# Sums of squares with tokens on partitions, a modulation in fewer operations, and a reordered end, in a two-layer decoder step

## What is computed

```python
def rmsnorm(x, g):
    xf = x.astype(jnp.float32)
    y = xf * lax.rsqrt(jnp.mean(xf * xf, axis=-1, keepdims=True) + EPS)
    return (y * g.astype(jnp.float32)).astype(x.dtype)

def modulate(h, shift, scale):
    return h * (1 + scale) + shift
```

## Time and profile before

| | us |
|---|---|
| runs | 1842.51, 1846.34, 1846.58 |
| median | 1846.34 |
| the profiled execution | 1857.14 |
| its span, first to last instruction | 1855.3 |
| TensorE busy | 1632.1 (88%) |
| VectorE busy | 802.2 (43%) |
| ScalarE busy | 675.4 (36%) |
| GpSimd busy | 141.8 (8%) |

### The profile page before, as it was taken

One profiled execution on the slowest core, in us unless ns is written; L12 is line 12 of the kernel. 1 busy time (PEld: TensorE's weight loads), 2 busy tenths in 40 slices (PEclk: granted clock), 3 DMA queues, 4 the chain that ended last, 5 costly groups with the idle time before them and its releaser, 6 DMA issues.

```text
span 1855.3 us, 31054 instructions
## 1 busy us (share of the span) xinstructions
PE 1632.1 (88%) x12244; PEld 1448.3 (78%) x12244; DVE 802.2 (43%) x1731; ACT 675.4 (36%) x1211; POOL 141.8 (8%) x273
## 2 busy tenths in 40 slices
PE   4698968889888999999999758999888999998996
PEld 3484457777477999998899637778577999998995
DVE  0234967677335333333353413443335333334433
ACT  2423223345214433334333323445314333334334
POOL 0311010111101000000000301111101000000000
PEclk9798569789798999999999878889888999999998
DMA  6514840002442544554131103002441222222211
GB/s 183 179 34 140 266 165 24 23 0 114 182 137 69 164 160 137 173 181 147 51 126 48 33 27 114 23 0 114 182 141 64 92 90 90 90 79 73 82 44 46
DMA packets 154361, 189.53 MB, mean 102 GB/s; under 512 B 6789, under 2 KB 148269, under 8 KB 149974
## 3 DMA queue, kind: packets, MB, share of 16 engines
q1 hardware_dynamic: 143906, 144.65, 24.5%
q0 software_dynamic: 5600, 36.24, 5.2%
q10 hardware_dynamic: 4768, 7.42, 1.2%
HBM read 183.65 MB, written 4.83 MB: 102 GB/s over the span
## 4 chain that ended last, share of the span: by engine, by line
PE 71%; DVE 12%; issue 8%; ACT 5%; DMA 2%; another core or an unknown queue 1%; ACTq 0%; DVEq 0%; POOL 0%; SPq 0%; POOLq 0%
PE ps L515 50%; PE ps L1033 3%; PE ps L1102 2%; DVE arena L949 2%; PE ps L1084 2%; DVE small L948 1%; PE ps L539 1%; PE ps L1052 1%; PE ps L598 1%; DVE arena L1263 1%; PE ps L1372 1%; PE ps L1318 1%; PE ps L1093 1%; DMA const<-in_const 1%
## 5 line engine op out<-in xcount | busy, mean ns | idle before, releaser
L515 PE MATMUL ps<-hH,wH 128*128 128x260 f32 x2592 | 535.9, 288 | 59.1 <-DVE hL L666 38.6
L515 PE MATMUL ps<-hL,wH 128*128 128x260 f32 x2592 | 529.6, 286 | 0.0
L515 PE MATMUL ps<-hH,wL 128*128 128x260 f32 x2592 | 529.6, 286 | 0.0
L515 PEld LDWEIGHTS ps<-hH,wH 128*128 128x128 f32 x2592 | 408.6, 193 | 67.1 <-issue 64.8
L499 DVE TENSOR_TENSOR wL<-ring,wH 128x1024 fp32r<-128x1024 f32 (+1 forms) x172 | 203.6, 1188 | 565.3 <-ACT wH L493 565.2
L515 PEld LDWEIGHTS ps<-hL,wH 128*128 128x128 f32 x2592 | 407.9, 192 | 0.0
L515 PEld LDWEIGHTS ps<-hH,wL 128*128 128x128 f32 x2592 | 407.5, 192 | 0.0
L493 ACT ACTIVATE wH<-ring 128x1024 fp32r<-128x1024 f32 (+1 forms) x184 | 188.8, 1029 | 584.5 <-PE ps L515 577.1
L1168 ACT ACTIVATE arena<-arena 128x128 f32<-128x128 f32 (+3 forms) x128 | 72.2, 564 | 190.2 <-DVE arena L1249 104.1
L1084 PE MATMUL ps<-arena 68*128 (+4 forms) x256 | 101.7, 488 | 8.1 <-DVE arena L1149 2.6
L1102 PE MATMUL ps<-arena 128*128 (+1 forms) x640 | 92.5, 279 | 14.9 <-ACT arena L1176 14.5
(11 more groups left out here) (258 smaller groups left out, 1804.3 us busy)
## 6 DMA issues: line engine op xcount, KB each, us to landing
ring<-in_w_ada SPq DMA_DIRECT2D x48, 1024.0 KB, 7.8
ring<-in_w_up SPq DMA_DIRECT2D x44, 1024.0 KB, 5.1
ring<-in_w_down SPq DMA_DIRECT2D x16, 1024.0 KB, 5.2
ring<-in_w_in_a SPq DMA_DIRECT2D x8, 1024.0 KB, 6.8
ring<-in_w_down SPq DMA_DIRECT2D x8, 768.0 KB, 4.6
ring<-in_w_in_b SPq DMA_DIRECT2D x6, 1024.0 KB, 5.3
ring<-in_w_o_a SPq DMA_DIRECT2D x4, 1024.0 KB, 7.8
ring<-in_w_o_b SPq DMA_DIRECT2D x4, 1024.0 KB, 10.2
```

Of the source, the lines that this page charges most:

```text
L515: ins = pe.matmul(ps[:, 2 * p + half, 0:HT], w[:, h, kc, t * P:t * P + P], mov[:, k0 + kc, half * HT:half * HT + HT], start=(first and kc ...
```

## The change

The sum of squares is turned round: a chunk's squares of 128 tokens are now the weights, and one column of ones moves, so the sums of 128 tokens land in one PSUM column, a token on each partition. 520 tokens take five such matmuls a chunk (`LANES`; the last lane overlaps). Root and reciprocal are of 128 x 5. `pe_spread` brings the reciprocals back to all partitions by multiplying with the identity. The modulation of the prompt tokens is one DVE operation with gain and reciprocal, then `hH` with the shift added on ScalarE, and `hL` in one DVE operation; the sample tokens of all chunks go together. The first panel goes chunk by chunk over both tiles. GpSimd's memsets and load are moved (`pool_fixed`): for n = 0 into the prologue, for n = 2 behind `pool_mod`. The split of the half of the second panel is issued inside the modulation (`ahead`). The residual of chunk 6 no longer waits for the last tile (`mid`). At the end GpSimd applies the gain to `xT` directly, TensorE transposes all of one half and then all of the other into seven banks, ScalarE and VectorE copy a half each with the reciprocal as scale, and SyncE stores from five buffers.

```diff
 def mm_half(pe, h, pairs, k0, nk, first, last, wait=None, mid=None):
+    if wait is None:
+        for t, p in enumerate(pairs):
+            ins = mm_tile(pe, h, t, p, k0, nk, first, last)
+            if t == 0 and mid is not None:
+                ins.then_inc(S(mid), 1)
+    else:
+        for kc in range(nk):
             wait(k0 + kc)
+            for t, p in enumerate(pairs):
+                ins = mm_chunk(pe, h, t, p, k0, kc, first and kc == 0, last and kc == nk - 1)
     ins.then_inc(S("w_used"), 1)
+LANES = (0, P, 2 * P, 3 * P, TOK - P)
 def pe_rms(pe, n, tiles=range(KC)):
     x_done(pe, n, 4)
     for kc in tiles:
+        if kc == 0:
+            pe.matmul(ps[:, 0, 0:5], zeros, ones[:, 0:5], start=True, stop=False)
         pe.wait_ge(S("rms_sq"), n * KC + kc + 1)
-        for half in range(2):
-            ins = pe.matmul(ps[:, half, 0:HT], ones[:, :], sq[:, kc % 2, half * HT:half * HT + HT],
-                            start=(kc == 0), stop=(kc == KC - 1))
+        for g, t0 in enumerate(LANES):
+            ins = pe.matmul(ps[:, 0, g:g + 1], sq[:, kc % 2, t0:t0 + P], ones[:, 0:1], start=False, stop=False)
+        if kc == KC - 1:
+            ins = pe.matmul(ps[:, 0, 0:5], zeros, ones[:, 0:5], start=False, stop=True)
         ins.then_inc(S("rms_sum"), 1)
+def pe_spread(pe, n):
+    pe.wait_ge(S("rms_ri"), n + 1)
+    for g in range(QT):
+        pe.matmul(ps[:, 6, g * P:g * P + P], rs[:, g:g + 1].to_broadcast([P, P]), ident, start=True, stop=True)
+    pe.matmul(ps[:, 7, 0:NS], rs[:, QT:QT + 1].to_broadcast([P, P]), ident[:, P - NS:P], start=True, stop=True).then_inc(S("rms_row"), 1)
 # act_rms, dve_rms
-    act.activation(v520(rt[:, :]), pair(0), ACT.Sqrt, bias=epsc[:, 0:1], scale=1.0 / D).then_inc(S("rms_rt"), 1)
-    dve.reciprocal(rt[:, :], rt[:, :]).then_inc(S("rms_ri"), 1)
+    act.activation(rs[:, 0:5], ps[:, 0, 0:5], ACT.Sqrt, bias=epsc[:, 0:1], scale=1.0 / D).then_inc(S("rms_rt"), 1)
+    dve.reciprocal(rs[:, 0:5], rs[:, 0:5]).then_inc(S("rms_ri"), 1)
+def act_mod(act, n, shift, ahead):
+    for kc in range(KC):
+        act.wait_ge(S("rms_t"), n * KC + kc + 1)
+        act.activation(hH[:, kc, 0:SEQ], hT[:, kc, 0:SEQ], ACT.Identity, bias=shift[:, kc, 0:1]).then_inc(S("rms_hi"), 1)
+        if kc == 0:
+            act.wait_ge(S("rms_s"), n + 1)
+            act.activation(hH[:, :, SEQ:TOK], hT[:, :, SEQ:TOK], ACT.Copy).then_inc(S("rms_his"), 1)
+        if kc == 6:
+            split_high(act, *ahead, 0)
+def dve_mod(dve, n, shift, ahead):
+    dve.wait_ge(S("rms_row"), n + 1)
+    dve.wait_ge(S("rms_mod"), n + 1)
+    dve.tensor_tensor(hT[:, :, SEQ:TOK], xT[:, :, SEQ:TOK], ps[:, 7, 0:NS].unsqueeze(1).to_broadcast([P, KC, NS]), ALU.mult)\
+        .then_inc(S("rms_ts"), 1)
+    for kc in range(KC + 2):
+        if kc < KC:
+            dve.scalar_tensor_tensor(out=hT[:, kc, 0:SEQ], in0=xT[:, kc, 0:SEQ], scalar=modA[:, kc, 0:1], in1=ps[:, 6, :],
+                                     op0=ALU.mult, op1=ALU.mult).then_inc(S("rms_t"), 1)
+        if kc >= 2:
+            u = kc - 2
+            dve.wait_ge(S("rms_hi"), n * KC + u + 1)
+            dve.scalar_tensor_tensor(out=hL[:, u, 0:SEQ], in0=hT[:, u, 0:SEQ], scalar=shift[:, u, 0:1], in1=hH[:, u, 0:SEQ].bitcast(F32),
+                                     op0=ALU.add, op1=ALU.subtract).then_inc(S("rms_lo"), 1)
+        if kc == 2:
+            dve.wait_ge(S("rms_his"), n + 1)
+            dve.tensor_tensor(hL[:, :, SEQ:TOK], hT[:, :, SEQ:TOK], hH[:, :, SEQ:TOK].bitcast(F32), ALU.subtract)\
+                .then_inc(S("rms_lo"), 1)
+        if kc == KC:
+            split_low(dve, *ahead, 0)
 # dve_out, dve_down: the residual of chunk 6
+            if m == KC - 2:
+                dve.wait_ge(S("o_mid"), l + 1)
+            else:
+                dve.wait_ge(S("w_used"), used(f"o{l}", 0, j - 1))
 # the end
+FIN_BANKS = (1, 2, 3, 4, 5, 6, 7, 1, 2, 3)
+def final_out(copy, eng, half):
+    eng.wait_ge(S("rms_ri"), 5)
+    for t in range(QT + 1):
+        n = 5 * half + t
+        eng.wait_ge(S("fi_t"), n + 1)
+        lo = 0 if t < QT else 96
+        copy(ytok[lo:P, t, half * 512:half * 512 + 512], ps[lo:P, FIN_BANKS[n], :], rs[lo:P, t:t + 1]).then_inc(S(f"fi_y{half}"), 1)
 # tensor
             for n in range(FIN_GROUPS):
+                half, t = n // 5, n % 5
+                bank = FIN_BANKS[n]
                 for k in range(4):
+                    kc = 4 * half + k
+                    pe.wait_ge(S("fi_x"), kc + 1)
+                    if n == 3:
+                        pe.wait_ge(S("dn1_free"), 4 + KC)
+                    if n >= 7:
+                        pe.wait_ge(S("fi_y0"), n - 6)
+                    ins = pe.transpose(ps[:, bank, k * P:k * P + P], hT[:, kc, LANES[t]:LANES[t] + P], ident)
+                ins.then_inc(S("fi_t"), 1)
 # gpsimd
+            for kc in range(KC):
+                pool.wait_ge(S("dn1_free"), 4 + kc + 1)
+                pool.tensor_scalar(hT[:, kc, :], xT[:, kc, :], vT[:, 32 + kc:33 + kc], None, ALU.mult).then_inc(S("fi_x"), 1)
```

More of the change, by code:

```diff
@@ L329, in build @@
         cvrow = part(FF)
[L331 to L332 removed]
+        ytok = part((QT + 1) * D, 0).rearrange("p (b d) -> p b d", b=QT + 1)
         def v520(a):
@@ L482, in _ @@
                         load_panel(sp, f"dn{l}", i, j, I["w_down"][l], *GROUPS[j // 2], (i * 2 + j % 2) * PC)
+            for t in range(QT + 1):
+                for half in range(2):
+                    sp.wait_ge(S(f"fi_y{half}"), t + 1)
+                if t < QT:
+                    sp.dma_start(O["y_p"][t * P:t * P + P, :], ytok[:, t, :]).then_inc(S("y_out"), 16)
+                else:
+                    sp.dma_start(O["y_s"], ytok[P - NS:P, t, :]).then_inc(S("y_out"), 16)
+            sp.wait_ge(S("stores"), 16 * STORES[3])
+            sp.wait_ge(S("y_out"), 16 * (QT + 1))
         def split_high(act, sec, i, j, h, nk=HK, cols=PC):
@@ L506, in half_ready, with mm_chunk, mm_tile, mm_half @@
                 pe.sem_inc(S(f"ring_free{s}"), 1)
-        def mm_tile(pe, h, t, p, k0, nk, first, last, wait=None):
-            for kc in range(nk):
-                if wait is not None:
-                    wait(k0 + kc)
-                for n, (w, mov) in enumerate(((wH, hH), (wH, hL), (wL, hH))):
-                    for half in range(2):
[L515 to L523, removed]
+        def mm_chunk(pe, h, t, p, k0, kc, first, last):
+            for n, (w, mov) in enumerate(((wH, hH), (wH, hL), (wL, hH))):
+                for half in range(2):
+                    ins = pe.matmul(ps[:, 2 * p + half, 0:HT], w[:, h, kc, t * P:t * P + P],
+                                    mov[:, k0 + kc, half * HT:half * HT + HT], start=(first and n == 0), stop=(last and n == 2))
+            return ins
+        def mm_tile(pe, h, t, p, k0, nk, first, last):
+            for kc in range(nk):
+                ins = mm_chunk(pe, h, t, p, k0, kc, first and kc == 0, last and kc == nk - 1)
+            return ins
+        def mm_half(pe, h, pairs, k0, nk, first, last, wait=None, mid=None):
+            if wait is None:
[5 more added lines that the diff above has]
+                for kc in range(nk):
+                    wait(k0 + kc)
+                    for t, p in enumerate(pairs):
+                        ins = mm_chunk(pe, h, t, p, k0, kc, first and kc == 0, last and kc == nk - 1)
             ins.then_inc(S("w_used"), 1)
@@ L754, in act_head @@
                     ahead = pn + 1 <= T[-1][0]
-                    if m0 == 0 and ahead:
+                    if m0 == 0 and ahead and pn:
                         split_high(act, sec, 0, pn + 1, 0, HK, head_cols(l, pn + 1))
@@ L787, in dve_head @@
                 if T[t][1] == 0 and pn + 1 <= T[-1][0]:
-                    for h in range(2):
+                    for h in range(0 if pn else 1, 2):
                         split_low(dve, f"head{l}", 0, pn + 1, h, HK, head_cols(l, pn + 1))
@@ L1555, in two @@
             def two(sec, i, q, k, nxt):
-                for h in range(2):
+                for h in range(1 if sec == f"{tag}h" else 0, 2):
                     split_high(act, sec, i, 2 * q + 1, h)
@@ L1612, in lows @@
             def lows(sec, i, j):
-                for h in range(2):
+                for h in range(1 if (sec, j) == (f"{tag}h", 1) else 0, 2):
                     split_low(dve, sec, i, j, h)
@@ L1752, in _ @@
                     pe.wait_ge(S("dn0_free"), 4 + KC)
+                pe_spread(pe, 2 * l)
                 pe_head(pe, l)
@@ L1766, in _ @@
                 pe_rms(pe, 2 * l + 1, range(HK, KC))
+                pe_spread(pe, 2 * l + 1)
                 pe_up(pe, l)
@@ L1912, in _ @@
                 dve_rms(dve, 2 * l + 2)
-            for kc in range(KC):
-                normed(dve, 4, kc)
-            phase_end(dve, "dve")
+            final_out(lambda out, x, r: dve.tensor_scalar(out, x, r, None, ALU.mult), dve, 1)
             phase_end(dve, "dve")
```

112 lines of the change are left out of this document (33 added, 79 removed).

## The result

| | before | after |
|---|---|---|
| median of the runs, us | 1844.66 (9 runs, 1840.29 to 1846.58) | 1852.39 (9 runs, 1846.38 to 1858.58) |
| ratio after / before | | 1.0042, 95% interval 1.0029 to 1.0055 |
| the profiled execution, its span | 1857.14, 1855.3 | 1846.50, 1844.6 |

The change makes the kernel 0.4% slower; 1852.8 was predicted. So I compare stage by stage, and look at the stretches between the stages apart.

The account below looks back on a forecast made before the run. TensorE, busy in 88% of the span, was taken to bound the kernel. Norms 0 to 3 and the end, +6.6 + 2.4 + 0.0 + 2.4 - 4.9 = +6.5 us, on 1846.3 gave 1852.8; own range 1848 to 1859.

Parts of the forecast that it names:

- The step on which the sign hung: TensorE's sums in all norms: one-column matmuls count as no work for the clock; 0.215 us an instruction at 1.2 GHz.
- Rival C: All norms: the one-column sums count as work throughout, so the clock holds and norm 0 rises as before; 1827, chance 0.08.
- Rival B: Clock outlives short stretches of sums, last half panels run whole, but no rise in the prologue; 1834.5, chance 0.13.
- Norm 0: Prologue to first product: sums and root +7.0, `ada0a` at the lower clock +1.7, moved GpSimd work -2.1; sum +6.6.
- Norms 1 and 3: Each +2.4: +3.0 before the gap, and the gap from product to product -0.6, 11.8 us against 12.4.
- the part ahead of the gap: Norms 1 and 3: first four sums +1.2, last half panel's restart 1.8; together +3.0 before the gap begins.
- Norm 2: As norm 1, but 2.5 us of waiting for the small load go away: 0.0, bounds -4.3 and +1.5.
- neither gains nor loses: First panel chunk by chunk: chunks follow each 1.34 us, TensorE takes 1.44 a chunk, so the order changes nothing.
- ready about 1 us before its turn, so nothing: Split issued ahead of chunk 7's `hL` waits for the first half panel, yet chunk 7 comes in time: no cost.
- Chunk 6's residual: Before the gap of norms 1 and 3: done 2.9 us earlier, but hidden by the sums of chunks 4 and 5.
- The end: Last product to end of span: 19 us, -7.9, plus +3.0 ahead of the gap: -4.9, bounds -10.6 and -2.
- Rival D: Last down-projection: GpSimd's eight products hold up VectorE's splits, for which TensorE waits; +10, 1857, chance 0.09.

Follow-up runs that it names:

- e1_wide: The changed kernel with each sum moving 128 columns of ones instead of one, and two PSUM banks cleared and closed: 1831.17 us, ratio 0.9935 to the kernel before.
- e5: The changed kernel with GpSimd's memsets and small load back ahead of the sample tokens' products: 1854.05 us, ratio 1.0061 to the kernel before.
- e3: The changed kernel with the first four sums of norms 1 and 3 as two pairs, ahead of each of the last two half panels: 1876.68 us, ratio 1.0171.
- e4: The changed kernel with the first panel tile by tile again, the split ahead kept: 1860.55 us, ratio 1.0077 to the kernel before.
- e6: The changed kernel with the residual of chunk 6 waiting for the whole panel again: 1853.63 us, ratio 1.0049 to the kernel before.
- e7: The changed kernel, chunk order kept, with the split of the second panel's first half behind the modulation again: 1853.79 us, ratio 1.0053 to the kernel before.
- e8: The changed kernel with the first panel tile by tile and the split behind the modulation again: 1849.97 us, ratio 1.0037 to the kernel before.
- e2_wide_keep: e1_wide plus five matmuls of 512 columns into an unused bank behind the spread of norms 1 to 3: 1826.76 us, ratio 0.9902 to the kernel before.
- e9_keep_all: e2_wide_keep with the five added matmuls behind the spread of norm 0 too: 1825.20 us, ratio 0.9890 to the kernel before.

## Why the prediction was right, and where it was not

**The clock.** The step on which the sign hung was that one-column sums neither raise nor hold the clock. It held in each of the five norms: the pace of 0.215 in norm 0, and half panels of 7.90, 8.00, 7.75 and 8.04 behind the sums of norms 1 to 4. e1_wide shows it by changing the number of columns (and the clearing that this needs). Rival C (busy time holds the clock) is refuted by a busy TensorE at a clock of 0.50. The Trainium skill (TensorE: Matmul & The Clock Gate, Part 1) ties the clock to how busy the engine has been; here an engine with matmuls back to back for 17.2 us stayed at the pace of 1.2 GHz. Rival B fell with the same half panels: 5.76 was its figure.

**Norm 0: +6.5, predicted +6.6**, and by the right terms. Start of the sums to start of `ada0a`: 11.03 before, 18.02 after, +7.0 as predicted. `ada0a` from there to its last product +2.2 (21.20 after, 19.05 before; predicted +1.7); from that product to the first head panel -2.6 (predicted -2.1), of which e5 gives 1.8 to GpSimd's order. That it fits to the tenth is luck: in e3, e4, e6, e7 and e8, which do the same here, the stage took 49.0 to 50.0 and not 50.43. In e6, e7 and e8 the clock rose for a while within `ada0a`; in the changed kernel it did not.

**Norms 1 and 3: +3.2 and +3.0, predicted +2.4.** The term that was too small is the part ahead of the gap, +3.9 instead of +3.0 (13.44 against 9.51). The first four sums took 5.54, where I had 4.95 (3.75 + 1.2). The 0.3 in it for sums that run slow stood on no row; the clock fell 2.4 us ahead of their end, and 5.54 is 1.1 more than the 4.47 that forty such instructions take at 2.4 GHz. And the half panel lost 2.14 instead of 1.8, nearly the whole price of a restart. The gap itself, product to product, went from 12.4 to 11.65; 11.8 was predicted. Inside it the spread took 2.3 (2.5 predicted), the modulation up to the first chunk 3.0 (as predicted). Chunk 7's `hL` was done at 599.5, 1.2 before its turn, as the text said.

**Norm 2: +0.4, predicted 0.0.** The size was right, the credit wrong. I gave 2.5 to moving the small load; e5 shows that with the load in its old place the new modulation hides all but 0.1 of it.

**Chunk order: "neither gains nor loses"** holds by itself (e8 against e7), but my sentence on the split ahead ("ready about 1 us before its turn, so nothing") was right only because of that order. The text named the two side by side and never asked what one is without the other: 1.2 to 1.3 us in each of four norms (e4 against e8).

**Chunk 6's residual** was costed at nothing, since the sums of chunks 4 and 5 hide it, and that held, though with little to spare. In the timeline of e6_no_mid the residual takes VectorE from 580.76 to 581.91 and its square ScalarE until 582.64, 2.0 us behind the product's end, where the sums of two chunks take 2.2; chunk 7's square is ready 3.2 behind it, where three take 3.4.

**The end: -3.6, predicted -4.9.** From the last product to the end 19.1 (19.0 predicted, 26.7 before). Of the 1.3 that are missing 1.1 are again the slow sums and half panel ahead of the gap: +4.1, not +3.0; the rest is the 26.9 that I had for before. The transposes took 5.13 for 24 (5.7 predicted), most of them at 1.2 GHz: there one takes 0.214, and not the 0.25 that I had. Rival D did not happen: GpSimd's eight products have 1.74 each instead of 1.3, but the stretch that holds the down-projection is as long as before (394.3 against 394.5).

**The sum.** The stages give +9.5, three above my sum, and yet the median came out at 0.4 from the prediction. Part of that is luck: I put +6.5 on 1846.3, and the runs have +7.7 on 1844.66. The stages of two single executions say +9.5; whether the change costs 7.7 or 9.5 I can't decide from them, since the stretches in between alone scatter by several us. The sign and the mechanism did not need that luck.

**What stays open.** e1_wide is 21.2 us faster than the changed kernel in the medians. In its five stages, each read from the matmul on zeros that opens it, it is 25.5 us faster (norm 0 8.5, norm 1 3.8, norm 2 4.1, norm 3 3.8, the end 5.4). The stretches between the stages, read the same way, add to 1657.6 us in e1_wide, to 1650.8 to 1659.0 in e5 to e8, and to 1647.5 in the changed kernel. So nothing here shows that e1_wide gives a part of its gain back there; it is the profiled execution of the changed kernel that has short stretches, as one that lies 5.9 below its median would. What makes these stretches scatter was not looked for.

## What to carry to other kernels

A rewrite that replaces wide matmuls by one-column ones can take away the work that held TensorE's clock, although the engine stays busy. Where each matmul has fresh weights, as here, moving 128 columns instead of one took no longer and kept TensorE at 2.4 GHz (1852 to 1831 us by one edit). Price a stretch of such work by what follows it as well: here the first four sums took 1.8 us longer and the half panel behind them 2.1. Before a difference of half a microsecond in a stage is put down to an edit, look at where the clock fell in the two traces (e6). Cost edits that lean on each other in all combinations, and not one after the other.

## What the runs showed of the hardware

The clock falls under a TensorE that is never idle: from 1.00 to 0.50 just behind 566 in the changed kernel, among forty one-column instructions back to back, and it doesn't rise through eighty (17.23 us; e5_pool_first reads 0.50 from 40 to 52). With 128 columns on the same weights it doesn't fall (norms 1 to 4 of e1_wide), and norm 0 runs at the pace of 2.4 GHz.

Transposes bring it back. At the end of the changed kernel TensorE makes nothing but transposes from 1830.94 on; its clock in windows:

```profile
1831.00:1834.00 3.00, 3.00 (x15) 0.50 0.03 5
1834.00:1836.00 2.00, 2.00 (x12) 0.55 0.00 0
1836.00:1838.00 2.00, 1.80 (x17) 1.00 0.08 31
```

The Trainium skill (TensorE: Matmul & The Clock Gate, Part 4) holds that a transpose doesn't count as busy in the same way. Here the clock was at 0.50, and rose to 1.00 under transposes alone; an instruction took 0.214 before the rise, and 0.112 in e1_wide, where all 24 ran at 1.00.

A 512-column matmul in f32 is two instructions of 0.44 each (ten in 4.39). In e2_wide_keep five such matmuls filled TensorE's wait for VectorE, and the clock stayed at 1.00 through it; in e9_keep_all they began at 0.50 (norm 0), took 5.1, and the clock rose within them.
